# First block of a two-block float32 transformer kernel: the order of its products, its loads and twelve products of zeros ahead

## The chip, the cores and the metric

The kernel runs on one core of a Trainium2 chip. The metric is device time in microseconds (us), lower is better. The kernel before took 2087.38 us (median of 3 runs, 2086.82 to 2088.19).

## The reference

Two transformer blocks for 512 tokens of width 1024, all in float32. The first (two layers) has a gated recurrence, a latent attention and an attention into 256 fixed memory tokens; the second has two feed-forward nets, a neighbourhood attention and a pooling branch. The change touches only the first work of the program, the keys of the memory tokens for layer 0:

```
def _memory_group(qm, mem, w_k, w_v):
    B, S, _ = qm.shape
    M = mem.shape[1]                                   # 256 memory tokens
    q = qm.reshape(B, S, MEM_HEADS, MEM_HDIM)
    k = (mem @ w_k).reshape(B, M, MEM_HEADS, MEM_HDIM) # the first block of products
    v = (mem @ w_v).reshape(B, M, MEM_HEADS, MEM_HDIM) # the second
    ...
```

## The kernel before

Each matrix product is made in three: both operands are split into an upper part (the float32 value rounded to fp32r) and a lower part (the rest), and TensorE adds upper x upper, upper x lower and lower x upper in PSUM. So each 128x512 tile of a weight is loaded into `raw`, cast by ScalarE into its upper part `wh`, and subtracted by GpSimd or VectorE into its lower part `wl`.

Weights come in *units* of four tiles (1 MB, 512 input rows by 512 columns). Units are numbered in the order in which TensorE uses them. Units 0 and 1 are `w_mk` of layer 0 (memory keys, 8 tiles, 4 banks of PSUM), units 2 and 3 are `w_mv` of layer 0 (memory values, 2 banks), 4 and 5 `w_mk` of layer 1, 6 and 7 `w_mv` of layer 1, and from 8 on the input projection. `raw` has two places (unit mod 2) and `wh`, `wl` have three (unit mod 3). The memory tokens arrive in four pieces of two row tiles; `mem_h`, `mem_l` are their upper and lower part and lie where `yh`, `yl` lie, so the trace calls them `yh` and `yl`.

The order on every engine is written out from one plan, and semaphores count the steps:

- SyncE (L955 to L980) issues the loads of weights. The load of unit u waits until all lower parts of unit u-2 are made, since these read `raw`. Unit 0 is loaded tile by tile, unit 1 in one piece; then come the five constant tables (ahead of unit 2), unit 2, the transposed input `x_t` (2 MB, ahead of unit 3) and unit 3.
- ScalarE casts: in `split_mem` (L1509) the first piece of memory tokens, tiles 0 and 1, the second piece, tiles 2 and 3, the third and fourth piece, then unit 1 (`high`, L1397, L1408). Later units are cast by `prepare` (L1428), two units ahead of TensorE.
- For units 0 to 7 the lower parts of tiles 0 and 2 are GpSimd's (L999) and those of tiles 1 and 3 are VectorE's (`low`, L1962). VectorE works strictly in its written order: the copies of finished banks (L1912), the lower parts two units ahead, and between the first and the second block a phase `setup` (L2017 to L2032, ten small operations on the gates' lower bounds), which stands behind the lower parts of unit 3 and ahead of those of unit 4.
- TensorE runs `piece` (L1049 to L1051) for each unit and bank: for each of four tiles the three products into that bank. In the first bank's piece each tile waits for its lower part before any of its products. So the first block is: unit 0 for banks 0, 1, 2, 3, then unit 1 for banks 0, 1, 2, 3, 96 products of 256 columns. The second block is 48 products of 512 columns, 24 for each unit.

Of the kernel before, what the change touches and what calls it, by code (L numbers as in the profile page):

```python
# [30 lines left out]
F32 = mybir.dt.float32  # L31
# [343 lines left out]
def build(nc, x, x_t, mem_t, positions, w_in, w_uq, w_uk, w_uv, w_mk, w_mv, w_out, ln_g, ln_b, cols_in,  # L375
# [3 lines left out]
    with ctx:  # L379
# [110 lines left out]
        small_loaded, const_loaded, x_loaded = sem("small_loaded"), sem("const_loaded"), sem("x_loaded")  # L490
        act_chain, dve_chain, stored = sem("act_chain"), sem("dve_chain"), sem("stored")
        mem_loaded = [sem(f"mem_loaded{i}") for i in range(4)]
        first_loaded = [sem(f"first_loaded{i}") for i in range(4)]
        xt_loaded = sem("xt_loaded")


# [408 lines left out]

        def raw_wait(eng, r):
            if r:
                eng.wait_ge(raw_loaded[r % 2], 16 * ((r + 1) // 2))


        def source_wait(eng, u):
# [42 lines left out]
        @block.sync  # L954
        def _(sp):  # L955
            for r, (b, src, _) in enumerate(raws):
                nk = src.shape[1]
                if r == 0:
                    for k in range(nk):
                        sp.dma_start(raw[:, 0, k, 0:b.width], b.w[:, k, :]).then_inc(first_loaded[k], 16)  # L960
                    continue
                if r == 2:
                    sp.dma_start(cols[:, :], cols_in).then_inc(const_loaded, 16)
                    sp.dma_start(ident[:, :], ident_in).then_inc(const_loaded, 16)
                    sp.dma_start(levels_raw, levels_in).then_inc(const_loaded, 16)
                    sp.dma_start(causal[:, :], causal_in).then_inc(const_loaded, 16)
                    sp.dma_start(pos_i[:, :], positions).then_inc(const_loaded, 16)
                if r == 3:
                    sp.dma_start(x_raw, x_t).then_inc(xt_loaded, 16)
                if r == 10:  # L970
                    sp.dma_start(xs[:, :, :], x.rearrange("(t p) n -> p t n", p=P)).then_inc(x_loaded, 16)

                if r >= 2:
                    user, _, u = raws[r - 2]
                    wait(sp, low_done, low_upto[u + 1][0])
                    wait(sp, low_done_dve, low_upto[u + 1][1])
                    if user.kind == "seven":

                        sp.wait_ge(sums_done, 4 * user.place + 4)
                sp.dma_start(raw[:, r % 2, 0:nk, 0:b.width], src).then_inc(raw_loaded[r % 2], 16)  # L980
            for t in range(T):
                for n in range(2):

                    sp.wait_ge(dve_step, finish.dve + 2 + 2 * t + n)
                    cut = slice(n * 512, (n + 1) * 512)
                    sp.dma_start(out[t * P:(t + 1) * P, cut], xs[:, t, cut]).then_inc(stored, 16)
            sp.wait_ge(stored, 16 * 2 * T)
# [13 lines left out]

        @block.tensor
        def _(pe):
            def piece(pc, half=None, ready=None):


# [21 lines left out]
                for k in range(nk):  # L1028
                    if j == 0:

                        pe.wait_ge(low_done_dve if low_on_dve(u, k) else low_done, low_at[u, k])
                    if u < 2 and j == 0 and k % 2 == 0:

                        pe.wait_ge(dve_step, (k0 + k) // 2 + 1)
                    if b.kind == "nat":
                        still = [o[:, b.k_from + k0 + k, cut] for o in (oh, ol)]
                        move = [w[:, u % 3, k, 0:b.width] for w in (wh, wl)]
# [16 lines left out]
                if b.ends(pc):  # L1054
                    mm.then_inc(bank_ready, 1)
                elif j == b.banks - 1:
                    mm.then_inc(unit_done, 1)

            def seven_piece(pc):

# [29 lines left out]
            for e in plan:  # L1090
                if isinstance(e, (Seven, Part)):
                    for pc in e.pieces():
                        seven_piece(pc)
                elif isinstance(e, Block):
                    for pc in half_pieces(e, 1) if e.begun else e.pieces():
                        piece(pc, half=1 if e.begun else None)
# [291 lines left out]
        def _(act):  # L1388
# [5 lines left out]
                ins.then_inc(act_chain, 1)  # L1394
                act.wait_ge(act_chain, chain[0])

            def high(u, ks=None):  # L1397
                if u >= len(units):
                    return
                b, k0, nk = units[u]  # L1400
                if u:
                    act.wait_ge(raw_loaded[u % 2], 16 * ((u + 1) // 2))

                units_over(act, u - 2)
                for k in ks or range(nk):
                    if u == 0:
                        act.wait_ge(first_loaded[k], 16)
                    act.copy(wh[:, u % 3, k, 0:b.width], raw[:, u % 2, k, 0:b.width]).then_inc(high_done, 1)  # L1408

            ahead = [2, 0]  # L1410
# [57 lines left out]
            for e in plan:  # L1468
# [40 lines left out]
                elif e.kind == "split_mem":  # L1509
                    for i in range(4):  # L1510
                        act.wait_ge(mem_loaded[i], 16)
                        act.copy(mem_h[:, 2 * i:2 * i + 2, :], mem_raw[:, 2 * i:2 * i + 2, :]).then_inc(act_step, 1)
                        if i < 2:
                            high(0, (2 * i, 2 * i + 1))
                    high(1)
                elif e.kind == "split_x":
                    act.wait_ge(xt_loaded, 16)
                    for i in range(e.first_head, e.first_head + 2):
# [260 lines left out]
        def _(dve):  # L1779
# [185 lines left out]
            def lows_behind(pc):  # L1965
# [6 lines left out]
                for k in range(-(-nk * j // b.banks), -(-nk * (j + 1) // b.banks)):  # L1972
                    if low_on_dve(u, k):
                        low(u, k)

            pending = []

            def read_pending(more=()):
# [6 lines left out]
            for e in plan:  # L1985
# [78 lines left out]
                elif e.kind == "split_mem":  # L2064
                    for i in range(4):
# [1 line left out]
                        dve.wait_ge(act_step, e.act + i + 1)  # L2067
                        step_done(dve.tensor_tensor(mem_l[:, cut, :], mem_raw[:, cut, :], mem_h[:, cut, :].bitcast(F32),
                                                    ALU.subtract))
                        if i < 2:  # L2070
                            low(0, 2 * i + 1)
                    low(1, 1)
                    low(1, 3)
                elif e.kind == "split_x":
                    for i in range(2):
                        cut = slice(2 * (e.first_head + i), 2 * (e.first_head + i) + 2)
# [444 lines left out]
```

## Time and profile before

| | before |
|---|---|
| median of 3 runs | 2087.38 us (2086.82 to 2088.19) |
| profiled execution, whole | 2087.4 us |
| its span, first to last instruction | 2085.6 us |
| TensorE busy | 2059.6 us, 99% |
| VectorE / ScalarE / GpSimd busy | 51% / 39% / 46% |
| mean granted TensorE clock | 0.999 |

All times below are us from the start of the span. A row of the timeline gives start, duration, engine, line and operation; what follows in brackets is the idle time before it and what ended it. TensorE's products overlap, so the distance between two starts, not the duration, is what one costs. A "landing" is the time from the issue of a DMA to its completion.

### The profile page before, as it was taken

The numbers are of one execution on the slowest core, as the hardware profiler recorded it, in microseconds if no ns is written. First come the engines' busy times: TensorE is split into PE (matmuls) and PEld (weight loads), VectorE is DVE, ScalarE is ACT, GpSimd is POOL, SyncE is SP. The second block draws the span as 40 slices with busy tenths as digits, with TensorE's granted clock in tenths as the row PEclk, the third lists the DMA queues.
The fourth block names the chain that finished last, engine by engine and source line by source line (L and its number), as shares of the span: only waits on it lengthen the run. The fifth ranks groups of instructions, "written<-read, shape, count | busy, mean of one in ns | idle before, by whom it ended". The sixth has DMA issues, their size and how long they took to land.

```text
span 2085.6 us, 33796 instructions
## 1 busy us (share of the span) xinstructions
PE 2059.6 (99%) x13712; PEld 1719.4 (82%) x13712; DVE 1059.5 (51%) x1861; ACT 819.4 (39%) x1665; POOL 949.9 (46%) x734
## 2 busy tenths in 40 slices
PE   8999999999999999999999999999999999999998
PEld 7878888778978888778888888888888898888886
DVE  6373565525464375534564554543432537544574
ACT  5424325554424235555523322344523433333245
POOL 5633434232443433232467666543445337676533
PEclk9999999999999999999999999999999999999999
DMA  7422223122321312213233223332132223333322
GB/s 277 156 64 81 79 68 102 41 82 63 100 83 61 98 59 77 68 54 106 63 119 121 93 90 101 112 126 93 61 114 89 81 81 121 101 122 102 101 74 89
DMA packets 98684, 196.69 MB, mean 94 GB/s; under 512 B 3680, under 2 KB 12256, under 8 KB 98144
## 3 DMA queue, kind: packets, MB, share of 16 engines
q1 hardware_dynamic: 95072, 183.25, 26.9%
q10 hardware_dynamic: 3456, 11.27, 1.6%
q8 instruction: 109, 1.79, 0.4%
q14 instruction: 47, 0.39, 0.1%
HBM read 192.41 MB, written 2.10 MB: 93 GB/s over the span
## 4 chain that ended last, share of the span: by engine, by line
PE 57%; ACT 1%; DVE 1%; DMA 0%; issue 0%; DVEq 0%; ACTq 0%
PE ps L1049 15%; PE ps L1051 15%; PE ps L1050 15%; PE ps L1077 3%; PE ps L1079 3%; PE ps L1078 3%; PE ps L1190 1%; PE ps L1330 1%; PE ps L1198 0%; PE ps L1207 0%; PE ps L1353 0%; PE ps L1373 0%; PE ps L1362 0%; PE ps L1243 0%; PE ps L1225 0%
## 5 line engine op out<-in xcount | busy, mean ns | idle before, releaser
L999 POOL TENSOR_TENSOR wl<-raw,wh 128x512 fp32r<-128x512 f32 (+2 forms) x676 | 878.3, 1324 | 1031.1 <-ACT wh L1428 1021.4
L1428 ACT CAST wh<-raw 128x512 fp32r<-128x512 f32 (+2 forms) x692 | 378.7, 604 | 606.7 <-PE ps L1051 440.5
L1049 PE MATMUL ps<-xh,wh 128*128 128x512 f32 (+1 forms) x1376 | 514.2, 374 | 1.7 <-issue 1.7
L1051 PE MATMUL ps<-xh,wl 128*128 128x512 f32 (+1 forms) x1376 | 508.7, 370 | 0.0
L1050 PE MATMUL ps<-xl,wh 128*128 128x512 f32 (+1 forms) x1376 | 508.5, 370 | 0.0
L1049 PEld LDWEIGHTS ps<-xh,wh 128*128 128x128 f32 x1376 | 259.3, 188 | 47.0 <-issue 4.5
L1051 PEld LDWEIGHTS ps<-xh,wl 128*128 128x128 f32 x1376 | 259.1, 188 | 44.5
L1050 PEld LDWEIGHTS ps<-xl,wh 128*128 128x128 f32 x1376 | 259.2, 188 | 42.0
L1049 PE MATMUL ps<-wh,xh 128*128 128x512 f32 (+1 forms) x608 | 238.9, 393 | 0.4 <-issue 0.4
L1050 PE MATMUL ps<-wl,xh 128*128 128x512 f32 (+1 forms) x608 | 234.5, 386 | 0.0
L1051 PE MATMUL ps<-wh,xl 128*128 128x512 f32 (+1 forms) x608 | 234.1, 385 | 0.0
L1877 DVE TENSOR_TENSOR side<-side,ps 128x512 f32<-128x512 f32 x124 | 84.2, 686 | 115.3 <-PE ps L1079 115.3
L1049 PEld LDWEIGHTS ps<-wh,xh 128*128 128x128 f32 x608 | 114.1, 188 | 23.0 <-issue 1.5
L1051 PEld LDWEIGHTS ps<-wh,xl 128*128 128x128 f32 x608 | 114.1, 188 | 21.6
L1050 PEld LDWEIGHTS ps<-wl,xh 128*128 128x128 f32 x608 | 114.2, 188 | 20.3 <-issue 0.2
L1049 PE MATMUL ps<-wh,yh 128*128 128x512 f32 x304 | 123.1, 405 | 1.2 <-ACT work L1451 1.2
L1051 PE MATMUL ps<-wh,yl 128*128 128x512 f32 x304 | 118.7, 390 | 0.0
L1050 PE MATMUL ps<-wl,yh 128*128 128x512 f32 x304 | 118.5, 390 | 0.0
L999 POOL TENSOR_TENSOR wl<-work,wh 128x512 fp32r<-128x512 f32 x54 | 71.8, 1350 | 79.9 <-ACT wh L1428 79.9
L1930 DVE TENSOR_TENSOR work<-ps,work 128x512 f32<-128x512 f32 x36 | 24.6, 689 | 160.3 <-PE ps L1051 160.3
L1428 ACT CAST wh<-work 128x512 fp32r<-128x512 f32 x54 | 32.0, 617 | 129.0 <-DVE work L1891 105.4
L1449 ACT ACTIVATE work<-ps 128x512 f32<-128x512 f32 x76 | 45.7, 601 | 73.9 <-PE ps L1051 73.8
(304 smaller groups left out, 2984.3 us busy)
## 6 DMA issues: line engine op xcount, KB each, us to landing
raw<-w_in SPq DMA_DIRECT2D x58, 1024.0 KB, 5.1
raw<-w_out SPq DMA_DIRECT2D x20, 1024.0 KB, 5.1
raw<-f1g SPq DMA_DIRECT2D x10, 1024.0 KB, 5.2
raw<-f1u SPq DMA_DIRECT2D x10, 1024.0 KB, 5.1
raw<-f1d SPq DMA_DIRECT2D x10, 1024.0 KB, 5.1
raw<-f2g SPq DMA_DIRECT2D x10, 1024.0 KB, 5.1
raw<-f2u SPq DMA_DIRECT2D x10, 1024.0 KB, 5.1
raw<-f2d SPq DMA_DIRECT2D x10, 1024.0 KB, 5.0
```

The lines of the kernel that those rows point to most:

```text
L999: pool.tensor_tensor(wl[s], source(u, k), wh[s].bitcast(F32), ALU.subtract).then_inc(low_done, 1)
L1049: pe.matmul(o, still[0], move[0], start=k0 + k == 0, stop=False)
L1050: pe.matmul(o, still[0], move[1], start=False, stop=False)
L1051: mm = pe.matmul(o, still[1], move[0], start=False, stop=k0 + k == b.ktiles - 1)
L1077: pe.matmul(o, sh, mh, start=k == 0 and s in CHAIN_FIRST, stop=False, skip_group_check=True)
L1078: pe.matmul(o, sh, ml, start=False, stop=False, skip_group_check=True)
L1079: mm = pe.matmul(o, sl, mh, start=False, stop=k == h - 1, skip_group_check=True)
L1190: mm = pe.matmul(ps[:, 4 + h, 0:width], q_heads[:, 2 * p + h, cut], k_heads[:, p, h, 0:width], start=True, stop=True)
L1428: act.copy(wh[:, v % 3, k, 0:width], source(v, k)).then_inc(high_done, 1)
L1449: ins = act.activation(b.arg[:, j, :], src, ACT.Silu)
L1877: ins = dve.tensor_tensor(dst, dst, src, ALU.add)
L1930: dve.tensor_tensor(hidden[:, j, :], src, SG[:, j, :], ALU.mult).then_inc(dve_evac, 1)
```

## The change

- TensorE's first block is made by `by_tiles`: tiles are taken in pairs; for both tiles of a pair the products with the upper part of the weights are made for all four banks (these need only `wh`), then those with the lower part for all four banks. The products are the same 96.
- Unit 1 is loaded tile by tile as unit 0, and ScalarE takes its tiles between the pieces of the memory tokens.
- The five constant tables are issued behind unit 2, together with `x_t`, not ahead of it.
- VectorE first clears one row tile of `xh`; TensorE then makes 12 products of 512 columns of these zeros into bank 7, which nothing has used yet.

```
                 nk = src.shape[1]
-                if r == 0:
+                if r < 2:
                     for k in range(nk):
-                        sp.dma_start(raw[:, 0, k, 0:b.width], b.w[:, k, :]).then_inc(first_loaded[k], 16)
+                        sp.dma_start(raw[:, r, k, 0:b.width], src[:, k, :]).then_inc(first_loaded[4 * r + k], 16)
                     continue
-                if r == 2:
+                if r == 3:
                     sp.dma_start(cols[:, :], cols_in).then_inc(const_loaded, 16)
...
+            pe.wait_ge(zeros_set, 1)
+            for _ in range(12):
+                pe.matmul(ps[:, 7, :], xh[:, 0, 0:P], xh[:, 0, :], start=True, stop=True)
...
+            def by_tiles(b):
+                oh, ol = operand[b.operand]
+                for pair in range(0, KD, 2):
+                    tiles = [(k, b.unit_ids[k // 4], k % 4) for k in (pair, pair + 1)]
+                    pe.wait_ge(dve_step, pair // 2 + 1)
+                    for k, u, kw in tiles:
+                        pe.wait_ge(high_done, tiles_upto[u] + kw + 1)
+                        for j in range(b.banks):
+                            still = wh[:, u, kw, j * P:(j + 1) * P]
+                            pe.matmul(ps[:, b.bank(j), 0:MEM_LEN], still, oh[:, k, 0:MEM_LEN], start=k == 0, stop=False)
+                            pe.matmul(ps[:, b.bank(j), 0:MEM_LEN], still, ol[:, k, 0:MEM_LEN], start=False, stop=False)
+                    for k, u, kw in tiles:
+                        pe.wait_ge(low_done_dve if low_on_dve(u, kw) else low_done, low_at[u, kw])
+                        for j in range(b.banks):
+                            mm = pe.matmul(ps[:, b.bank(j), 0:MEM_LEN], wl[:, u, kw, j * P:(j + 1) * P],
+                                           oh[:, k, 0:MEM_LEN], start=False, stop=k == KD - 1)
...
                     for i in range(4):
                         act.wait_ge(mem_loaded[i], 16)
                         act.copy(mem_h[:, 2 * i:2 * i + 2, :], mem_raw[:, 2 * i:2 * i + 2, :]).then_inc(act_step, 1)
-                        if i < 2:
-                            high(0, (2 * i, 2 * i + 1))
-                    high(1)
+                        high(i // 2, (2 * (i % 2), 2 * (i % 2) + 1))
...
+            dve.memset(xh[:, 0, :].bitcast(F32), 0.0).then_inc(zeros_set, 1)
...
                         step_done(dve.tensor_tensor(mem_l[:, cut, :], mem_raw[:, cut, :], mem_h[:, cut, :].bitcast(F32),
                                                     ALU.subtract))
-                        if i < 2:
-                            low(0, 2 * i + 1)
-                    low(1, 1)
-                    low(1, 3)
+                        low(i // 2, 2 * (i % 2) + 1)
```

SyncE's queue at the start of the program, before; `w_mk` 128x512 is a tile of unit 0, 128x4x512 the whole of unit 1, and the two `w_mv` are units 2 and 3:

```order
L960 DMA raw<-w_mk 128x512 x4
L980 DMA raw<-w_mk 128x4x512
L963 DMA cols<-cols_in 128x177
L964 DMA ident<-ident_in 128x128
L965 DMA work<-levels_in 128x192
L966 DMA causal<-causal_in 128x512
L967 DMA pos_i<-positions 128x4
L980 DMA raw<-w_mv 128x4x512 [waits low_done_dve,low_done]
L969 DMA work<-x_t 128x4096
L980 DMA raw<-w_mv 128x4x512 [waits low_done_dve,low_done]
```

The same queue in the changed kernel:

```order
L961 DMA raw<-w_mk 128x512 x8
L981 DMA raw<-w_mv 128x4x512 [waits low_done_dve,low_done]
L964 DMA cols<-cols_in 128x177
L965 DMA ident<-ident_in 128x128
L966 DMA work<-levels_in 128x192
L967 DMA causal<-causal_in 128x512
L968 DMA pos_i<-positions 128x4
L970 DMA work<-x_t 128x4096
L981 DMA raw<-w_mv 128x4x512 [waits low_done_dve,low_done]
```

The five tables have moved from ahead of unit 2's wait to behind its load; `x_t` and unit 3 stand behind them now.

TensorE's first rows before, the first bank's piece of unit 0 (`yh`, `yl` are the memory tokens):

```order
L1049 MATMUL ps<-yh,wh 128x256 [waits dve_step,low_done]
L1050 MATMUL ps<-yl,wh 128x256
L1051 MATMUL ps<-yh,wl 128x256
L1049 MATMUL ps<-yh,wh 128x256 [waits low_done_dve]
L1050 MATMUL ps<-yl,wh 128x256
L1051 MATMUL ps<-yh,wl 128x256
```

TensorE's first rows now, the zeros and the start of the first pair; the second piece shown is the end of that pair:

```order
L1008 MATMUL ps<-xh 128x512 [waits zeros_set]
L1008 MATMUL ps<-xh 128x512 x11
L1072 MATMUL ps<-yh,wh 128x256 [waits high_done,dve_step]
L1073 MATMUL ps<-yl,wh 128x256
...
L1077 MATMUL ps<-yh,wl 128x256 [waits low_done]
L1077 MATMUL ps<-yh,wl 128x256 x3
L1077 MATMUL ps<-yh,wl 128x256 [waits low_done_dve]
L1077 MATMUL ps<-yh,wl 128x256 x3
```

The first real product now waits for an upper part, and the lower parts are asked for sixteen products later. On VectorE the rows from the copies of the first banks to the lower parts of unit 4 stand as before.

## Rows read from the trace of the kernel before

**Rows 1.** The page, part 1: busy us, share of the span, instructions.

```profile
PE 2059.6 (99%) x13712; PEld 1719.4 (82%) x13712; DVE 1059.5 (51%) x1861; ACT 819.4 (39%) x1665; POOL 949.9 (46%) x734
```

**Rows 2.** Waits of TensorE, whole span: us in total, times, longest.

```profile
PE ps L1049 <- POOL wl L999: 8.2, 2, 7.6
```

**Rows 3.** Timeline of TensorE, the first three blocks of products.

```profile
7.55 0.58 PE L1049 MATMUL ps<-yh,wh 128*128 128x256 f32 x1 [7.55 <-POOL wl L999]
...
9.83 0.58 PE L1049 MATMUL ps<-yh,wh 128*128 128x256 f32 x1 [0.63 <-POOL wl L999]
...
14.27 0.38 PE L1051 MATMUL ps<-yh,wl 128*128 128x256 f32 x1
14.48 0.29 PE L1049 MATMUL ps<-yh,wh 128*128 128x256 f32 x1
...
22.75 0.40 PE L1049 MATMUL ps<-wh,yh 128*128 128x512 f32 x1
...
33.66 0.28 PE L1049 MATMUL ps<-yh,wh 128*128 128x256 f32 x1
...
34.01 0.28 PE L1049 MATMUL ps<-yh,wh 128*128 128x256 f32 x1
```

**Rows 4.** Timeline of ScalarE: casts of the upper parts.

```profile
5.54 1.26 ACT L1408 CAST wh<-raw 128x512 fp32r<-128x512 f32 x2
...
8.97 0.62 ACT L1408 CAST wh<-raw 128x512 fp32r<-128x512 f32 x1 [0.74 <-DMA raw<-w_mk]
...
16.19 2.18 ACT L1428 CAST wh<-raw 128x512 fp32r<-128x512 f32 x4 [1.99 <-DMA raw<-w_mv]
23.80 2.18 ACT L1428 CAST wh<-raw 128x512 fp32r<-128x512 f32 x4 [5.42 <-DMA raw<-w_mv]
```

**Rows 5.** Timeline of SyncE's queue: issues of the loads.

```profile
0.74 1.81 SPq L960 DMA_DIRECT2D raw<-w_mk  x4
...
10.42 0.38 SPq L980 DMA_DIRECT2D raw<-w_mv  x1
10.84 0.51 SPq L969 DMA_DIRECT2D work<-x_t  x1
16.32 0.38 SPq L980 DMA_DIRECT2D raw<-w_mv  x1
```

**Rows 6.** DMA issues, 0 to 60 us: count, KB each, median us to landing.

```profile
work<-x_t SPq DMA_DIRECT2D x1, 2048.0 KB, 10.2
...
causal<-causal_in SPq DMA_DIRECT2D x1, 256.0 KB, 8.0
```

**Rows 7.** The page, part 6: loads of one unit elsewhere.

```profile
raw<-w_out SPq DMA_DIRECT2D x20, 1024.0 KB, 5.1
```

**Rows 8.** Windows: busy of PE, PEld, DVE, ACT, POOL, clock, DMA share, GB/s.

```profile
12.00:14.00 2.00, 2.00 (x11) 2.00 (x11) 0.80 (x1) 1.97 (x4) 1.28 (x2) 1.00 1.00 347
...
16.00:18.00 2.00, 2.00 (x19) 2.00 (x18) 0.88 (x2) 1.81 (x4) 1.11 (x1) 1.00 1.11 475
```

**Rows 9.** Timeline of GpSimd: lower parts of unit 3.

```profile
24.50 3.00 POOL L999 TENSOR_TENSOR wl<-raw,wh 128x512 fp32r<-128x512 f32 x2 [4.61 <-ACT wh L1428]
```

**Rows 10.** Timeline of VectorE: memory tokens, unit 3, a row of `setup`, unit 4.

```profile
5.66 0.69 DVE L2068 TENSOR_TENSOR yl<-work,yh 128x512 fp32r<-128x512 f32 x1 [5.66 <-ACT yh L1512]
...
24.97 1.37 DVE L1962 TENSOR_TENSOR wl<-raw,wh 128x512 fp32r<-128x512 f32 x1 [3.87 <-ACT wh L1428]
...
27.97 0.15 DVE L2020 TENSOR_TENSOR stat<-cols 128x8 f32<-128x8 f32 x1
...
32.01 1.29 DVE L1962 TENSOR_TENSOR wl<-raw,wh 128x512 fp32r<-128x512 f32 x2
```

**Rows 11.** The end: TensorE's last product, then windows as in Rows 8.

```profile
2077.90 0.39 PE L1051 MATMUL ps<-wh,yl 128*128 128x512 f32 x1
```

**Rows 12.** Windows around the fall of the clock, columns as in Rows 8.

```profile
2082.00:2083.00 1.00, 0.00 (x0) 0.00 (x0) 1.00 (x2) 0.00 (x0) 0.00 (x0) 0.98 1.01 383
2083.00:2084.00 1.00, 0.00 (x0) 0.00 (x0) 0.11 (x1) 0.00 (x0) 0.00 (x0) 0.50 0.83 313
```

More of the change, by code:

```diff
@@ L492, in build @@
         mem_loaded = [sem(f"mem_loaded{i}") for i in range(4)]
-        first_loaded = [sem(f"first_loaded{i}") for i in range(4)]
+        first_loaded = [sem(f"first_loaded{i}") for i in range(8)]
+        zeros_set = sem("zeros_set")
         xt_loaded = sem("xt_loaded")
@@ L907, in raw_wait @@
             if r:
-                eng.wait_ge(raw_loaded[r % 2], 16 * ((r + 1) // 2))
+                eng.wait_ge(raw_loaded[r % 2], 16 * (r // 2))
         def source_wait(eng, u):
@@ L1031, in piece @@
                         pe.wait_ge(low_done_dve if low_on_dve(u, k) else low_done, low_at[u, k])
-                    if u < 2 and j == 0 and k % 2 == 0:
-                        pe.wait_ge(dve_step, (k0 + k) // 2 + 1)
                     if b.kind == "nat":
@@ L1057, in piece @@
                     mm.then_inc(unit_done, 1)
+            def by_tiles(b):
[14 more added lines that the diff above has]
+                                           oh[:, k, 0:MEM_LEN], start=False, stop=k == KD - 1)
+                            if k == KD - 1:
+                                mm.then_inc(bank_ready, 1)
+                            elif k == 3 and j == b.banks - 1:
+                                mm.then_inc(unit_done, 1)
             def seven_piece(pc):
@@ L1093, in _ @@
                         seven_piece(pc)
+                elif isinstance(e, Block) and e.unit_ids[0] == 0:
+                    by_tiles(e)
                 elif isinstance(e, Block):
@@ L1395, in link, with high @@
                 act.wait_ge(act_chain, chain[0])
[L1397 to L1407, printed above, removed]
+            def high(u, ks):
+                b = units[u][0]
+                for k in ks:
+                    act.wait_ge(first_loaded[4 * u + k], 16)
                     act.copy(wh[:, u % 3, k, 0:b.width], raw[:, u % 2, k, 0:b.width]).then_inc(high_done, 1)
```

## The prediction

> **What bounds the kernel now.** I read part 1 of the page first: TensorE is busy for 2059.6 of 2085.6 us [rows 1], so a gain can only come from its idle time or from products that run slowly. The table of its waits puts most of the idle time in one place: 8.2 us behind a lower part from GpSimd, 7.6 of it in one wait [rows 2], and the timeline shows that this is the start of the program. The first product starts at 7.55, a second wait of 0.63 us ends at 9.83, and the products follow 0.21 us apart (14.27 to 14.48, for 256 columns) until 14.48 [rows 3]. From 14.48 to 22.75 the other 69 of the 96 products take 8.27 us, 0.120 each. That is the change between the two levels of the clock, 1.2 and 2.4 GHz, though the granted clock is shown as 1.00 in the windows on both sides of it [rows 8]. So the start holds two costs: TensorE begins late, and its first 27 products run at half rate.
>
> Then I asked what would stop TensorE if the first block ended earlier, and read the other engines' timelines up to 34 us. Unit 3 is the late one. ScalarE waits 5.42 us for it and casts it at 23.80 [rows 4]; its first lower part starts at 24.50 [rows 9] and, with 1.5 us for one (3.00 for two), is ready at 26.0. TensorE comes to it at 22.75 + 5.46 = 28.2, as the second block's 48 products take 33.66 - 22.75 = 10.91 us. That slack of 2.2 us is all that TensorE can gain there while unit 3 arrives when it does. One unit later the slack is smaller: VectorE makes the lower part of tile 1 of unit 4 from 32.01, two in 1.29 us, so it is ready at 32.7 [rows 10], and TensorE uses it at 34.01 [rows 3]. Slack there: 1.3 us. VectorE is late because it works in order: lower part of unit 3 at 24.97, two more bank copies and another lower part, `setup` from 27.97, then unit 4 [rows 10]. This chain, 23.80 to 32.7, is 8.9 us long and hangs on nothing but the landing of unit 3.
>
> **The change part by part.**
>
> The zeros. 12 products of 512 columns at half rate cost 12 x 0.427 (twice the 0.213 of 256 columns) = 5.1 us. The engines issue their first work at 0.74 [rows 5] and a clear of one tile should take no longer than a lower part without a rival for the memory, 0.7 us (1.29 for two [rows 10]). So they run from about 1.4 to 6.5. Before, TensorE did nothing there.
>
> The first block. The first upper parts are cast from 5.54 [rows 4], and the first lower part of the memory tokens is over at 5.66 + 0.69 = 6.35 [rows 10], so the first pair can start behind the zeros, at about 6.5, at full rate if the zeros have raised the clock: 96 x 0.120 = 11.5 us, end at 18.0 if no tile is late. The last tile of each pair comes in time: each pair takes 2.9 us, and ScalarE needs three casts of 0.62 for it, 1.9 us. Local gain: 22.75 - 18.0 = 4.75 us. If the clock isn't raised, 27 products at half rate cost 2.5 us more and the end is 20.5.
>
> Unit 2. Its load is issued when unit 0's lower parts are done, at 10.42 as before [rows 5], because nothing ahead of it changes. A unit's load with nothing ahead of it lands in 5.1 us [rows 7], so at 15.5, against a cast at 16.19 before [rows 4]. Its first lower part is ready by 17.6. No wait.
>
> Unit 3, the step that decides. Before, the time from unit 2's cast to unit 3's, 16.19 to 23.80, was 7.6 us for `x_t` and unit 3, 3 MB, with the DMA engines full all the time; that unit 3 was issued at 16.32 [rows 5] and `x_t` landed at 10.84 + 10.2 = 21.0 [rows 6] says that unit 3 just stood in the line. Now the line behind unit 2 is the constants, `x_t` and unit 3. The constants are 0.5 MB (`causal`, the half of them, 0.25 [rows 6]); at the 347 GB/s of the window in which they moved before [rows 8] they take 1.5 us. Unit 3 lands at 15.5 + 1.5 + 7.6 = 24.6, 0.8 later than before. The reason is plain: the same bytes must pass before unit 3, and they now leave a hole between the last tile of unit 1 and unit 2. Bounds: no hole at all gives 23.8; two more microseconds, if the small tables go badly by themselves and leave another hole ahead of `x_t`, give 26.6. I take 24.6.
>
> TensorE then ends unit 2 at 18.0 + 5.46 = 23.4, and waits for unit 3's first lower part until 24.6 + 2.2 = 26.8. The wait is 3.4 us and eats the gain of the first block down to 28.2 - 26.8 = 1.4. Unit 3 ends at 32.3. With the clock not raised by the zeros the wait is shorter and unit 3 starts at the same 26.8, so here the zeros are worth nothing.
>
> Unit 4. The chain on VectorE gives its tile 1 at 24.6 + 8.9 + 0.05 = 33.5. TensorE would be there at 26.8 + 5.46 + 0.35 = 32.6 and waits 0.9 us more. Against 34.01 before that leaves 0.5 us. Behind it TensorE is never short: unit 5 is free to be loaded when unit 3's lower parts are done and, with 5.1 us to land, 0.6 for the cast and 1.5 for a lower part, is ready 2 us and more ahead of its use. From there the program runs on as before, shifted by what is left.
>
> The constants' wait ahead of the second block costs nothing: five issues of about 0.5 us each (as `x_t`'s, 0.51 [rows 5]) end at 13.5, and by the same line they land by 15.5 + 1.5 = 17.0, ahead of 18.0. Were they a microsecond later still, the wait would come off the one ahead of unit 3.
>
> Sum: 0.5 to 0.6 us less. The profiled execution took 2087.4 (span 2085.6 and 1.8 around it), which is the median of the runs, so I expect 2086.8.
>
> **The rivals.**
>
> *The whole local gain stays*, 4.8 us: 2082.6. For it speaks the idle and slow time in the first 14 us. It needs unit 3 landed by 21.2, 2.6 us earlier than before with the same bytes in the line. 6%.
>
> *No hole*: unit 3 lands at 23.8 as before, the constants costing nothing extra because the engines moved 475 GB/s in places [rows 8]. The bound is then VectorE's chain alone, 1.3 us: 2086.1. 22%.
>
> *Unit 3 lands later than 25.1*: from there VectorE's chain ends later than 34.01 and the change loses, up to 1.5 us at 26.6: middle 2088.1. 12%.
>
> *The clock falls in the new wait ahead of unit 3* (the one on the other side that depends on TensorE). It was full until 4.7 us after the last product at the end of the program: last product over at 2078.3 [rows 11], clock down at 2083.0 [rows 12]. My wait is 3.4 us, shorter, but near. If it fell, the 24 products of unit 3 would start at half rate; before, it rose 6.9 us after the first product and 4.65 after the wait that ended at 9.83 [rows 3], so half of 4.65 to 6.9, 2.3 to 3.5 us, is lost, 0.9 of which the wait for unit 4 hides. Against before: 0.9 to 2.1 us slower, 2088.9. It decides from a wait about as long as the one at the end. 10%.
>
> The Trainium skill (TensorE: Matmul & The Clock Gate, "HAM oscillation — how this bites in real kernels") has this as its warning: bursts of products with waits for DMA between them start each time at the low clock. By that rule the wait ahead of unit 3 makes the change a loss; the trace has no such wait in the middle, and its end speaks for a clock that holds somewhat longer.
>
> *My forecast*, 50%.
>
> **The numbers.** Forecast and likeliest case 2086.8. The runs of before spread by 1.4 us, so each case carries 0.7 on each side. The range of 8 in 10 reaches from the no-hole case less its spread, and a little for parts I can't see, to the case of the fallen clock: 2084.4 to 2089.2. About 0.2%, 4.2 us, is what a measurement of this kernel can tell from no change. Only the whole gain passes it: faster 0.06. Slower by as much needs a late unit 3 and a fallen clock together, or something I haven't seen: 0.03. Within: 0.91.
>
> **What would show it.** Zeros from about 1.4 to 6.5, then products 0.12 us apart from the first pair on, and the first block over near 18.0. A wait of about 3.4 us on TensorE ahead of unit 3, near 23.4, ended by GpSimd; a cast of unit 3 at about 24.6; a second wait, below 1 us, for VectorE at 33.5; the third block of products, at 33.66 before, at 32.3. If unit 3 lands by 21 or TensorE shows no wait at 23.4, I'm wrong on the line of loads; if the products of unit 3 start 0.43 us apart, on the clock.

## The result: 3.2 us slower

The changed kernel takes 2090.39 us (median of 22 runs, 2089.57 to 2091.49), the kernel before 2087.20 (22 runs, 2086.21 to 2088.67): 3.2 us slower, ratio 1.0014 with a 95% interval of 1.0008 to 1.0021. The forecast was 2086.8. The profiled execution took 2090.33, close to the median, with a span of 2088.5. A few single executions of 3456 to 5216 us are left out of all medians below, the profiled one of run 15 (4184 us) among them.

TensorE's timeline answers to [rows 3]; it shows the zeros, the first real product, the first product of the second block, of unit 3 (behind the wait), one of unit 3 at the low clock, and the first and fourth of the third block:

```profile
1.45 4.89 PE L1008 MATMUL ps<-xh 128*128 128x512 f32 x12 [1.45 <-DVE xh L1994]
6.77 0.39 PE L1072 MATMUL ps<-yh,wh 128*128 128x256 f32 x1 [0.43 <-DVE yl L2088]
...
18.37 0.43 PE L1052 MATMUL ps<-wh,yh 128*128 128x512 f32 x1
...
28.46 0.50 PE L1052 MATMUL ps<-wh,yh 128*128 128x512 f32 x1 [4.15 <-POOL wl L1000]
...
30.84 0.63 PE L1053 MATMUL ps<-wl,yh 128*128 128x512 f32 x1
...
35.67 0.28 PE L1052 MATMUL ps<-yh,wh 128*128 128x256 f32 x1
...
36.02 0.28 PE L1052 MATMUL ps<-yh,wh 128*128 128x256 f32 x1
```

The first block does what it should: it starts at 6.77 at full rate and is over at 18.37, 4.4 us earlier than at 22.75. Then TensorE waits 4.15 us for GpSimd's first lower part of unit 3, and unit 3 itself takes 35.67 - 28.46 = 7.21 us instead of 5.44. The third block starts 2.0 us late. ScalarE's casts of units 2 and 3 and SyncE's queue say why unit 3 is late (they answer to [rows 4] and [rows 5]):

```profile
16.19 2.18 ACT L1448 CAST wh<-raw 128x512 fp32r<-128x512 f32 x4 [3.22 <-DMA raw<-w_mv]
26.45 2.18 ACT L1448 CAST wh<-raw 128x512 fp32r<-128x512 f32 x4 [8.08 <-DMA raw<-w_mv]
```

```profile
10.84 0.38 SPq L981 DMA_DIRECT2D raw<-w_mv  x1
11.26 0.51 SPq L964 DMA_DIRECT2D cols<-cols_in  x1
...
13.79 0.43 SPq L970 DMA_DIRECT2D work<-x_t  x1
15.44 0.38 SPq L981 DMA_DIRECT2D raw<-w_mv  x1
```

The windows, columns as in [rows 8], show the hole in the loads from 10 to 14 (GB/s last; 372 and 347 before) and the clock (third from last) falling while unit 3 is multiplied:

```profile
10.00:12.00 2.00, 2.00 (x19) 2.00 (x18) 1.91 (x3) 1.98 (x5) 1.36 (x2) 1.00 0.54 190
12.00:14.00 2.00, 2.00 (x19) 2.00 (x18) 2.00 (x2) 0.97 (x2) 1.99 (x2) 1.00 0.87 249
...
28.00:30.00 2.00, 1.54 (x6) 1.19 (x6) 2.00 (x4) 0.62 (x2) 2.00 (x2) 0.85 0.02 7
30.00:32.00 2.00, 2.00 (x6) 1.55 (x5) 1.50 (x7) 0.94 (x3) 0.25 (x2) 0.50 0.25 15
32.00:34.00 2.00, 2.00 (x8) 1.59 (x8) 1.97 (x2) 1.34 (x3) 2.00 (x2) 0.80 0.81 240
```

The fall of the clock is the rule for this kernel and not a chance of one execution: the mean granted clock is 0.998 or 0.997 in 20 of its 22 executions, and 0.999 or 1.000 in every one of the kernel before in the sets below.

VectorE, as in [rows 10], is held by the same landing. Its lower parts of unit 4 come at 34.61 instead of 32.01:

```profile
27.62 1.34 DVE L1980 TENSOR_TENSOR wl<-raw,wh 128x512 fp32r<-128x512 f32 x1 [6.52 <-ACT wh L1448]
...
34.61 1.28 DVE L1980 TENSOR_TENSOR wl<-raw,wh 128x512 fp32r<-128x512 f32 x2
```

So tile 1 of unit 4 would have been ready at 35.25, 1.24 us later than TensorE used it before, whatever the clock; the fall of the clock adds the other 0.77 to the 2.01. From there to the end another 0.9 us is lost (last product at 2080.82, 2077.90 before); where, the experiments on the zeros show in part.

### The profile page after: what moved, and what is told of

The parts are those of the page before. It is cut to its first block, busy times and chain, and to the rows that moved or that the text cites. A ratio compares the mean times of both kernels' runs of the same rounds, so it can differ in the third digit from the quotient of the medians.

```text
span 2088.5 us, 33824 instructions
## 1 busy us (share of the span) xinstructions
PE 2064.2 (99%) x13724; PEld 1721.5 (82%) x13724; DVE 1063.0 (51%) x1862; ACT 819.4 (39%) x1665; POOL 951.0 (46%) x734
## 3 DMA queue, kind: packets, MB, share of 16 engines
q10 hardware_dynamic: 3456, 11.27, 1.6%
## 4 chain that ended last, share of the span: by engine, by line
PE 57%; ACT 1%; DVE 1%; DMA 0%; issue 0%; DVEq 0%; ACTq 0%
PE ps L1052 15%; PE ps L1054 15%; PE ps L1053 15%; PE ps L1103 3%; PE ps L1102 3%; PE ps L1104 3%; PE ps L1217 1%; PE ps L1357 1%; PE ps L1225 0%; PE ps L1234 0%; PE ps L1380 0%; PE ps L1400 0%; PE ps L1389 0%; PE ps L1270 0%; PE ps L1252 0%
## 5 line engine op out<-in xcount | busy, mean ns | idle before, releaser
L1948 DVE TENSOR_TENSOR work<-ps,work 128x512 f32<-128x512 f32 x36 | 24.6, 689 | 159.7 <-PE ps L1054 159.7
```

What stands on the lines that cost most here:

```text
L1948: dve.tensor_tensor(hidden[:, j, :], src, SG[:, j, :], ALU.mult).then_inc(dve_evac, 1)
```

## The experiments

Theory A: the landing of unit 3 decides (a hole in the line of loads), then VectorE's chain, then the clock. Rivals: B, the split of unit 1 slows the queue; C, the order by pairs slows products; B', the fall of the clock is the whole loss; later D and F, the zeros cost something long after they ran; E, this late cost comes from the place of TensorE's instructions in its stream, which the zeros move. "Shift" is how much later than in the one trace of before the 401st real product starts (81.05 us there), behind all that the change touches. "Difference" is the median (10 to 12 runs) less the median of the kernel before beside it (2087.78, 2087.44, 2087.54, 2087.74 and 2087.42 in the five sets). The ratio's interval is about 0.0009 wide on each side, so a single difference below 1.9 us is not clear by itself: only those of the changed kernel and of runs 11 and 12 are. The traces carry most readings, and each is of one execution.

| kernel | unit 3 cast at | shift | difference |
|---|---|---|---|
| changed | 26.45 | +2.01 | +3.2 |
| 1 constants ahead | 25.01 | +0.01 | +0.8 |
| 2 and x_t behind unit 3 | 20.38 | -2.08 | -0.7 |
| 3 no zeros | 26.49 | +1.88 | +1.2 |
| 4 zeros in the wait | 26.01 | +1.04 | +1.5 |
| 5 before again | 25.02 | +0.06 | -0.2 |
| 6 before, zeros | 24.80 | -0.17 | +1.0 |
| 7 x_t behind unit 5 | 20.97 | -2.00 | -1.8 |
| 8 before, constants late | 26.46 | +1.49 | +0.9 |
| 9 before, 24 zeros | 24.82 | +0.99 | +0.7 |
| 10 as 7, 24 zeros | 20.30 | -2.11 | -1.2 |
| 11 as 7, no zeros | 20.99 | -2.12 | -3.1 |
| 12 changed, 24 zeros | 26.92 | +3.76 | +2.6 |
| 13 before, clear only | 25.68 | +0.72 | +0.2 |
| 14 before, zeros, clear on GpSimd | 25.28 | +0.88 | +0.6 |
| 15, 17 before, pairs only (cast and shift of run 17) | 25.04 | +0.61 | -0.4, -0.2 |
| 16 before, x_t behind unit 5 | 21.71 | -0.01 | -0.3 |
| 18 before, pairs and x_t behind unit 5 | 21.68 | -0.91 | -1.4 |

**1. Constants ahead.** The changed kernel with the tables where they were.

```
-                if r == 3:
+                if r == 2:
                     sp.dma_start(cols[:, :], cols_in).then_inc(const_loaded, 16)
```

> The changed kernel with one edit: the five constant tables are issued ahead of unit 2 again, not behind it. Theory A (the line of loads decides: a hole of about 1.5 us between the last tile of unit 1 and unit 2 made unit 3 land at 26.45 instead of 23.80, and VectorE's chain of 8.9 us behind it sets the third block): the hole is filled, unit 3 is cast at 23.8 to 24.3, TensorE waits 1.9 to 2.4 us ahead of it, the clock stays up, tile 1 of unit 4 starts at 32.7 to 33.2 (34.01 in the kernel before, 36.02 in the changed one), so 2.8 to 3.3 us faster than the changed kernel, near 2087.4. Theory B (the split of unit 1 into four loads slows the queue, wherever the constants stand): unit 3 is cast after 25.5 and at most 1 us is gained. Theory C (the order by pairs or the zeros make later products slower): no more than 1 us gained although unit 3 lands early.

Unit 3 was cast 1.4 us earlier, not 2.4, TensorE waited 2.57 us for it and 0.48 for VectorE, the clock stayed up in the trace, and 2.0 us of the start came back (the whole of its loss). The median is above the 2087.4 that was expected. Part of that is the clock: 8 of the 11 executions have a mean of 0.998, so in most of them it must have fallen on the way, though not in the one that the trace shows. B predicts a late unit 3 here too, and 25.01 looks like it, until run 5.

**5. The kernel before, again** (no edit).

> The kernel before, word for word, once more. The changed kernel and two kernels of the first set that hold the zeros end 0.7 to 0.9 us later than their start says (the shift of TensorE's products against the one trace of before is +2.01 at 56 us and +2.92 at the end in the changed kernel), the one without zeros does not. This run shows how far two traces of one kernel drift apart. Theory A (that is the noise of single executions, and the loss is all in the first 35 us): a drift of up to 0.9 us here too, and the same median as before. Theory D (the zeros, or the instructions they add, cost 0.8 us much later): less than 0.3 us here.

Its unit 3 was cast at 25.02, and tile 1 of unit 4 started at 33.97 (34.01 in the other trace of this kernel).

```profile
25.02 2.18 ACT L1428 CAST wh<-raw 128x512 fp32r<-128x512 f32 x4 [6.68 <-DMA raw<-w_mv]
```

In the seven traces of runs 1, 5, 6, 9, 13, 14 and 17, all with constants and `x_t` in their old places, it was cast at 24.80 to 25.68, in that of run 15 at 24.13. The 23.80 of [rows 4], the base of the forecast, was the earliest of nine. With 25.0 the split of unit 1 costs nothing: run 1 and run 5 agree, B falls. Between 81 us and the end this trace gains 0.59 us on the other one of the same kernel (0.85 at the product at 2045 us alone), so the late part of a single trace says little by itself.

**8. The kernel before with the constants late**, the reverse of edit 1.

> The kernel before with the constants issued behind unit 2, nothing else. Theory A: the hole between unit 1 and unit 2 alone makes unit 3 land 1 to 2 us later, at 25 to 26; TensorE, which wants it at 28.2, does not notice, but VectorE's chain of 8.9 us behind it gives tile 1 of unit 4 at 33.9 to 34.9 instead of 32.7, against 34.01: 0 to 0.9 us slower than before. Theory B (it is the split of unit 1 into four loads that makes unit 3 late): unit 3 lands at 23.8 to 24.3 and the time is that of before.

Unit 3 at 26.46 as in the changed kernel, and tile 1 of unit 4 at 35.41, behind 0.48 us of waiting for VectorE:

```profile
26.46 1.67 ACT L1428 CAST wh<-raw 128x512 fp32r<-128x512 f32 x3 [8.44 <-DMA raw<-w_mv]
...
35.41 0.39 PE L1049 MATMUL ps<-yh,wh 128*128 128x256 f32 x1 [0.48 <-DVE wl L1962]
```

Against run 5 the tables' new place alone costs 1.4 us of landing and as much at the start, with no zeros and no fall of the clock. A holds.

**2. x_t behind unit 3** as well as edit 1.

```
-                if r == 3:
+                if r == 4:
                     sp.dma_start(x_raw, x_t).then_inc(xt_loaded, 16)
```

> As the first of this set, and the transposed input x_t (2 MB) is issued behind unit 3 instead of ahead of it. Theory A: unit 3 is issued at about 15.4 and lands in about 5 us, its cast at 20.5 to 21; TensorE, done with unit 2 at 23.8, doesn't wait; VectorE's chain ends at 29.5 to 30, near the time at which TensorE wants tile 1 of unit 4 (29.6). Nearly the whole gain of the first block, 4.4 us, is kept as far as that, less up to 1 us if unit 4 now stands behind x_t: 2083 to 2084.5, 6 to 7.5 us faster than the changed kernel. Theories B and C: the waits go, but the total stays above 2086.

Unit 3 was ready before TensorE was (24.00), as expected, but unit 4, now behind `x_t`, was cast only at 28.30 and cost two waits, 0.82 and 0.51 us. Of 4.4 us, 2.1 stayed, and the median says 0.7, with executions between 2086.01 and 2090.86; the profiled one is the second fastest. That is far from the 2083 to 2084.5 expected, and above the 2086 that was to speak for B or C, so it is the trace that speaks for A here, not the time.

**3. No zeros** in the changed kernel: clear, wait and 12 products taken out.

> The changed kernel without the clear and the 12 products of zeros. Theory A: the first block runs at half rate up to some 6 us after its start and ends at 20.5 to 21 instead of 18.4, unit 3 lands as late as in the changed kernel (26.45), so TensorE starts it at the same 28.5, after a wait of 1.5 to 2 us in which the clock does not fall; unit 3 takes 5.5 us, and VectorE's chain lets tile 1 of unit 4 start at 35.3 instead of 36.0. So 0.7 us faster than the changed kernel: about 2089.7. Theory B' (the clock's fall is the whole loss): about 1.8 us faster or more. If the zeros were of use as meant: slower than the changed kernel by about 2 us.

First block over at 20.18, unit 3 at the same 28.5, and 1.2 above before instead of 3.2, so about 2 us faster, with the two kernels measured in different sets. But the wait was 2.70 us and the clock fell in it (0.56 and 0.59 in the windows below), so the start gained only 0.13; the rest came later. The expectation, 0.7 us, all at the start and with the clock up, was wrong in size, in place and on the clock. The size is that of B', but B' asks for a clock that stays up, and it fell here too.

```profile
28.50 0.80 PE L1048 MATMUL ps<-wh,yh 128*128 128x512 f32 x1 [2.70 <-POOL wl L1000]
```

```profile
28.00:30.00 2.00, 1.50 (x4) 1.21 (x5) 2.00 (x4) 0.67 (x2) 2.00 (x2) 0.56 0.02 7
30.00:32.00 2.00, 2.00 (x7) 1.58 (x6) 1.50 (x7) 0.91 (x3) 0.25 (x2) 0.59 0.06 12
```

**4. Zeros in the wait**, 14 more products of zeros ahead of unit 3.

```
+                if u == 3 and j == 0:
+                    for _ in range(14):
+                        pe.matmul(ps[:, 5, :], xh[:, 0, 0:P], xh[:, 0, :], start=True, stop=True)
```

> The changed kernel, with 14 more products of zeros (512 columns, into an unused bank) ahead of unit 3's first product, 3.2 us of work in the wait of 4.15 us. Theory A: the clock stays up, unit 3 (28.46 to 33.9) takes 5.5 instead of 7.2 us, but tile 1 of unit 4 then waits for VectorE until 35.3 (36.02 in the changed kernel): 0.7 us faster, about 2089.7. Theory B' (the clock's fall is the whole loss): 1.75 us faster, 2088.6. If the clock falls nonetheless: no change.

The clock held in the trace, unit 3 took 5.9 us, and then VectorE's chain took over, as A says:

```profile
24.07 3.33 PE L1030 MATMUL ps<-xh 128*128 128x512 f32 x14
28.04 0.50 PE L1055 MATMUL ps<-wh,yh 128*128 128x512 f32 x1 [0.64 <-POOL wl L1000]
...
34.95 0.39 PE L1055 MATMUL ps<-yh,wh 128*128 128x256 f32 x1 [0.48 <-DVE wl L1983]
```

Tile 1 of unit 4 at 34.95 against 36.02: 1.07 us, of which unit 3's earlier landing (26.01) explains 0.44 and the clock 0.6. The clock held in all 11 executions (mean 0.999 or 1.000), and still the start is 1.04 us late and the median 1.5 above before. So B' falls: at the start the clock is the smaller part. The medians alone (1.7 us less than the changed kernel, where A said 0.7 and B' 1.75) would not decide it; the wait for VectorE does.

**6, 9. Zeros alone** ahead of the old first block, 12 of 512 columns and 24 of 256.

```
+            pe.wait_ge(zeros_set, 1)
+            for _ in range(12):
+                pe.matmul(ps[:, 7, :], xh[:, 0, 0:P], xh[:, 0, :], start=True, stop=True)
```

> The kernel before with the clear and the 12 products of zeros alone. Both theories: the first block starts at 7.55 as before, but at full rate, and ends near 20 instead of 22.75; unit 3 still lands at 23.8, so TensorE waits from 25.5 to 26.0 and is then held by VectorE's chain: tile 1 of unit 4 at 32.7 instead of 34.0. Theory A: 1.3 us faster than before. Theory D: only 0.5 us faster, with a drift of 0.7 to 0.9 us between 60 us and the end.

> The kernel before with the clear and 24 products of zeros of 256 columns instead of 12 of 512: the same 5 us of work at the start, but TensorE's instructions (a load of weights and a product each) are moved by 48 places instead of 24. With 12 the start gained 0.2 us and the median lost 0.95; 0.4 us of it appeared in one place at 1354 us and more ahead of the product at 2045 us. Theory E (the place of TensorE's instructions in its stream decides, by how they are fetched): the place at 1354 us is as in the kernel before, and the median moves by more than 0.4 us, to within 0.5 us of before. Theory F (zeros ahead cost about 1 us later for another reason): the median stays 0.8 to 1.2 us above before.

Both medians are above before, where run 6 was expected 1.3 or 0.5 us below. In the trace of run 6 the first block ended 1.6 us earlier and 0.2 us of it was left behind VectorE's chain. In that of run 9 it ended 0.8 us *later*: the clock rose early, but between the zeros and the real products TensorE waits 1.2 us, and 1.1 more before tile 2, and the clock fell again for most of the block:

```profile
4.00:6.00 2.00, 2.00 (x12) 2.00 (x12) 0.13 (x1) 0.78 (x2) 0.00 (x0) 1.00 1.01 353
8.00:10.00 2.00, 0.93 (x6) 0.59 (x5) 1.02 (x3) 1.00 (x3) 1.72 (x1) 0.82 1.05 405
10.00:12.00 2.00, 1.96 (x9) 1.96 (x10) 1.74 (x3) 0.86 (x3) 0.00 (x0) 0.50 1.08 378
12.00:16.00 4.00, 4.00 (x21) 4.00 (x21) 2.84 (x2) 2.17 (x4) 2.98 (x2) 0.50 1.11 397
```

The trace of run 14, with 12 products, shows the same (waits of 1.49 and 1.10 us, 0.50 from 10 to 16, first block over at 23.63), while that of run 6 had such waits too (1.46 and 1.11) and kept its clock. The mean clock of each execution tells which is the rule: of run 6's eleven, nine are at 0.998 or 0.997, the profiled one at 1.000 is the exception, and the kernel before has 0.999 or 1.000.

**7, 10, 11. x_t behind unit 5** (`if r == 6:`), constants ahead; with 12 zeros, with 24, and without.

> The changed kernel with the constants ahead of unit 2 and x_t issued behind unit 5 (in the second kernel of the first set it stood behind unit 3, and unit 4 was cast at 28.30, so that TensorE waited 0.8 and 0.5 us for it). Theory A: unit 3 is cast at 20.4, unit 4 at about 26, the third block starts at about 29.5 (33.66 before) without a wait, and 4.1 to 4.4 us are gained there; x_t lands at about 35, well ahead of its use. Total 3.3 to 4.3 us faster than before. If the queue of loads is only stretched further (unit 6 behind x_t lands after 41): waits ahead of unit 6 and a gain of less than 3 us.

> The kernel with the constants ahead of unit 2 and x_t behind unit 5 (2085.67 us), with 24 products of zeros of 256 columns instead of 12 of 512. Theory E: 0.4 to 1 us faster than that, 2084.7 to 2085.3. Theory F: the same, 2085.7.

> The same kernel without clear and zeros. The first block then ends at 20.2 instead of 18.5, so the third block starts at 31.2 instead of 29.9 (33.66 before), 2.5 us early; GpSimd's lower parts of unit 8 let only 2.0 us of any gain through at 56 us. So the zeros are worth nothing there, and without their cost later: 2084.7 to 2085.3, as fast as or faster than with them (2085.67). If the zeros are worth what they save at the start: 2086.5 to 2087.

Run 7 was expected 3.3 to 4.3 us faster than before and is 1.8; run 11 came out a little below its 2084.7 to 2085.3. Run 7 kept 3.8 us up to unit 8 and lost 1.8 there, to GpSimd, which makes all four lower parts of unit 8 while VectorE makes those of `x_t` (one lower part took up to 2.28 us, the median 1.29). Three waits, of which two:

```profile
53.50 0.51 PE L1052 MATMUL ps<-xh,wh 128*128 128x512 f32 x1 [0.18 <-POOL wl L1000]
...
54.74 0.50 PE L1052 MATMUL ps<-xh,wh 128*128 128x512 f32 x1 [0.27 <-POOL wl L1000]
```

Run 11, without zeros, reaches that gate with 2.95 us in hand and leaves it with the same 2.1. It is the fastest kernel here, 2084.43 against 2087.54 (ratio 0.9986, 0.9977 to 0.9995), and beats the kernels with zeros, runs 7 and 10. Here the zeros are worth nothing at the start and cost 1.3 us (against run 7, in another set) to 2.0 (run 10, in the same) later, with the clock up in nearly every execution of all three.

**12. The changed kernel with 24 zeros.**

> The changed kernel with 24 products of zeros of 256 columns instead of 12 of 512. Unit 3 still lands at 26.0 to 26.5, TensorE waits about 4 us and its clock falls in most executions: the shift at 56 us is 1 to 2 us against before, as in the changed kernel. Theory E: without the loss later, the median is 1 to 2 us above before instead of 3.2. Theory F: 2.7 to 3.2 us above before.

Unit 3 at 26.92, the clock low for longer in this trace (third block at 37.42), the median 2.6 above before, near the 2.7 of F. In runs 9, 10 and 12 TensorE's instructions were meant to be moved by 48 places instead of 24, and the zeros cost the same. By the words of the expectations that speaks against E; the next runs take the force out of it.

**13, 14. The clear alone, and the clear on GpSimd.**

> The kernel before with VectorE's clear of one tile alone, 0.48 us at 0.9 us from the start, where VectorE is idle; no products of zeros. If the clear (one instruction more ahead of all others on VectorE) brings the late loss: the start is as before (shift at 80 us between 0 and 0.1 us), the 0.36 us at 1354 us and -0.28 at 1746 appear, and the median is 0.5 to 1 us above before. If the products bring it: nothing at those places, and the time of before.

> The kernel before with the 12 products of zeros, the tile cleared by GpSimd instead of VectorE. With the clear on VectorE the start gained 0.2 us and the median lost 0.95. If VectorE's clear brings the late loss: nothing at 1354 and 1746 us, and the median within 0.3 us of before or below it. If the products bring it: the two places as in the other kernels with zeros and 0.8 to 1.1 us above before.

Run 13 is 0.2 us above before, run 14 0.6: neither is clear by itself, but both lean to the products as the cause. All ten traces whose clear is on VectorE (runs 1, 2, 4, 6, 7, 9, 10, 12, 13 and the changed kernel) have 0.36 us more at 1354 us, where eight transposes wait for their first weight load; none of the others has. Run 13 has it, without products:

```profile
1354.98 0.42 PEld L1331 LDWEIGHTS ps<-ident,work 128*128 128x128 f32 x4 [0.43 <-issue]
1355.01 1.23 PE L1331 MATMUL ps<-ident,work 128*128 128x128 f32 x8
```

and run 14, with products, has not:

```profile
1354.70 1.02 PEld L1336 LDWEIGHTS ps<-ident,work 128*128 128x128 f32 x8
1354.89 1.07 PE L1336 MATMUL ps<-ident,work 128*128 128x128 f32 x8
```

At 1746 us a gain of 0.28 goes with the products of zeros (it is in run 14, not in 13), though the traces of runs 17 and 18, which have neither, show 0.28 and 0.21 too; that place is not settled. The larger late loss is at the product at 2045 us. It waits for ScalarE, which waits for two loads one behind the other, `post_gains` and `p_t`. From 2042 us to there the shift against the trace of before falls by 0.47 to 1.05 us in all eight other traces without zeros, and changes by -0.39 to +0.50, 0.16 on average, in the ten with them. The trace of before itself stands with these ten because its `p_t` took 4.24 us, more than in any other. `post_gains` landed in 4.7 us in the changed kernel:

```profile
work<-post_gains ACTq DMA_DIRECT2D x1, 512.0 KB, 4.7
```

and in 3.5 in run 16:

```profile
work<-post_gains ACTq DMA_DIRECT2D x1, 512.0 KB, 3.5
```

It took 4.21 to 4.80 us in all ten traces with products of zeros and 3.29 to 3.91 in all nine without, 1.0 us less on average. So the loss goes with the products, not with the clear.

The traces show one thing more that goes with them. Each holds a single packet of 16 KB in the queue of instructions near this load. It starts 0.9 to 1.3 us after the issue of `post_gains` in all ten traces with products of zeros, in the midst of the load, and 3.7 to 3.9 us after it in all nine without, when the load is over or nearly so. The first two lines (packets, MB, share of the engines) are the changed kernel's queues in the 3 us from the issue of `post_gains`, 2034.5 to 2037.5; the third is all that run 16 has in its 3 us, 2032.3 to 2035.3:

```profile
q10 hardware_dynamic: 133, 0.49, 40.4%
q8 instruction: 1, 0.02, 3.1%
...
q10 hardware_dynamic: 138, 0.52, 51.7%
```

So the zeros do seem to cost by their place in the stream of instructions: they bring a load of instructions forward into a load of data that TensorE's chain waits for. The test by 48 places did not move that packet away (1.0 to 1.3 us behind the issue in runs 9, 10 and 12, 1.0 to 1.2 with 12 products in runs 1, 2, 6, 7, 14 and the changed kernel), so it could not refute E. That the one packet makes the other load 1.0 us longer is argued from 19 traces, and no run moved it alone.

**15, 17, 16, 18. The order by pairs alone, x_t behind unit 5 alone, and both.**

> The kernel before with the first block's order by pairs alone; unit 1 in one piece, constants ahead of unit 2, no zeros. The first block starts at 6.5 instead of 7.55 and ends near 20.5 instead of 22.75. Unit 3 lands at 23.8 to 25.0, so TensorE starts it at 26.0 to 27.2 after a wait of 0 to 1.2 us, and VectorE's chain gives tile 1 of unit 4 at 32.7 to 33.9 (34.01 before): 0.1 to 1.3 us faster at 56 us, with no late loss: 0 to 1.3 us faster than before. Rival (order by pairs slows the products): slower than before.

> The kernel with the order by pairs alone once more, for its trace. The median was 2087.5 against 2087.74, no difference. Theory A: the first block ends near 20.5, TensorE waits 0.5 to 1.5 us for unit 3 and for tile 1 of unit 4 up to 33.1 to 33.9, so the shift at 80 us is -0.1 to -0.9: the gain of 2 us of the first block is gone by then.

> The kernel before with x_t issued behind unit 5 instead of ahead of unit 3, nothing else. Unit 3 lands at 21.5 or earlier, but TensorE wants it only at 28.2 and did not wait for it before: no gain from it, the shift at 56 us 0 to 0.1, the time of before within 0.4 us. Rival (the later load itself brings the gain of 3.1 us of the kernel without zeros): 1 us faster or more.

> The kernel before with two edits: the order by pairs and x_t issued behind unit 5; unit 1 in one piece. Theory A: the first block ends at about 20.5 (its last tiles come from one load that lands at 12.0, early enough), unit 3 is there before TensorE is, and the third block starts at 31.4 instead of 33.66; the lower parts of unit 8 let 2.0 us through: 2 to 3 us faster than before, within 0.6 us of the kernel that also splits unit 1 (2084.43 against 2087.54). If the split of unit 1 is needed: less than 1.5 us.

Alone, each edit is worth nothing that can be told from no change: by pairs the first block is over at 20.93, and unit 3 (0.53 us) and VectorE (0.48 us) take the gain. Another 0.5 us is lost at unit 8, at 58.58, where TensorE waits for GpSimd, which the expectation for run 17 (a shift of -0.1 to -0.9) had left out:

```profile
27.09 0.50 PE L1049 MATMUL ps<-wh,yh 128*128 128x512 f32 x1 [0.53 <-POOL wl L999]
...
33.98 0.39 PE L1049 MATMUL ps<-yh,wh 128*128 128x256 f32 x1 [0.48 <-DVE wl L1986]
```

while with `x_t` later unit 3 is cast at 21.71 and nobody has use for it. Together they give 1.4 us (2.7 at the third block, 0.9 behind unit 8; the interval of the ratio, 0.9987 to 1.0005, holds no change), and with unit 1 in four and its tiles cast earlier 3.1 (run 11). By the expectation for run 18 less than 1.5 us says that the split of unit 1 is needed. C falls: the products by pairs are 0.12 us apart like the others.

## Why the prediction was wrong

- *The zeros and the first block.* Right: zeros from 1.45 to 6.3, first product at 6.77, 0.12 us apart, end at 18.37 (18.0 forecast); local gain 4.4 us (4.75).
- *Unit 2.* Slightly off: issued at 10.84, not 10.42, since VectorE's lower part of tile 3 took 0.99 us, and cast at 16.19, not 15.5. The 15.5 used 5.1 us from loads elsewhere, while this load took 5.75 in the trace of before and 5.33 here. No harm to TensorE, but the next sum starts from it.
- *Unit 3, the step that decides.* Right in kind, mis-sized: "Unit 3 lands at 15.5 + 1.5 + 7.6 = 24.6", measured 26.45. The 1.5 for the constants was right: run 8 shows 1.4. The other two terms were low. The 7.6 is a time from cast to cast, so it belonged behind the cast of unit 2 at 16.19 and not behind a landing at 15.5 (0.7 us). And it was short: from cast to cast it is 7.6 in the one trace of before and 8.6 to 9.2 in the seven traces of runs 1, 5, 6, 9, 13, 14 and 17. With run 5's 8.9 the same sum gives 16.2 + 1.5 + 8.9 = 26.6. My upper bound was 26.6, so the case lay in the stated range of the landing, and I gave all beyond 25.1 only 12%.
- *The base.* The slack of 2.2 and 1.3 us was read from the same execution, in which unit 3 came at 23.80; it usually comes near 25.0, where VectorE's chain leaves nothing. So even the no-hole case would have gained nothing, as runs 1 and 17 show. This is the first error: one execution's row was taken as the kernel's.
- *The clock.* I held it safe because it had stayed up 4.7 us behind the last product [rows 11, 12] and my wait was 3.4. The wait became 4.15, and the clock fell (0.50 from 30 to 32). Run 3 shows that a shorter wait would not have been safe either: 2.70 us, and it was down by then. One observation of how long a clock holds is no lower bound. The Trainium skill's warning (TensorE: Matmul & The Clock Gate, "HAM oscillation — how this bites in real kernels") described what came. Its price here was 0.77 us, since VectorE's chain hid 1.0 of the 1.77 that unit 3 took longer. I had priced it at 1.4 to 2.6 us against my own case, so the term was too large and its chance of 10% too small.
- *"Here the zeros are worth nothing".* Wrong in sign: kernels that hold them lose about 1 us behind the start, most of it ahead of the product at 2045 us. The prediction put everything behind the start at nothing ("From there the program runs on as before").
- *The sum.* Tile 1 of unit 4 was forecast at 33.5 and came at 36.02. Of these 2.5 us 1.75 are the landing (ready at 35.25) and 0.77 the clock. Two rivals, the late unit 3 (up to 1.5 us, which fits) and the fallen clock, were treated as exclusive but for 3%. They share a cause: the later unit 3, the longer the wait. Together, 2.0 at the start, with 0.9 later, they pass the range, whose end of 2089.2 was set by one of them, with 0.3 of the 0.7 of spread above its 2088.9.

## What to carry to other kernels

Before an engine is sped up, find what the next stage's data wait for: here a queue of loads that ran full, so that an earlier first block became a longer wait; the gain came only when 2 MB that nobody needed yet were moved behind the loads that were needed (run 11). Tables issued ahead of a load that must wait for a buffer are free filling for the queue; moved behind it they leave a hole and then stand in the way. Rivals with one cause belong together in a range, and slacks under 2 us need more than one trace. And instructions added at the start can move a load of instructions 2 ms later into a load that counts; the traces show it next to `post_gains`, though no run has tried to move it back.

## What was not expected of the hardware

Products of zeros raised the clock before the first real product in the changed kernel (0.12 us apart from there on), in the trace of run 4 only four products later (0.21 us apart up to 7.58). But a high clock reached early was lost again behind waits of 1.2 to 1.5 and 1.1 us, so that the block behind them ran slower than with no zeros (runs 9 and 14, first block over at 23.59 and 23.63 against 22.75), though not in the trace of run 6 with the same waits. The profile shows a granted clock of 1.00 up to its first change, also while products are 0.21 us apart [rows 3, 8]. A clear of 0.48 us on an idle VectorE at the start of the program moved a stall of 0.36 us into a place 1350 us later, in all ten traces that hold it; why, no run tells. And a load of 0.5 MB took 1.0 us longer on average where one packet of instructions fell into it.
